# Gated recurrence: score products of a head woven with the output projection of the head in front

## What is computed

```python
def step(S, xs):                      # block by block, per head
    qb, kb, vb, gb = xs
    G = jnp.cumsum(gb, axis=2)
    diff = G[:, :, :, None, :] - G[:, :, None, :, :]
    decay = jnp.exp(jnp.where(tri[:, :, None], diff, -jnp.inf))
    A = jnp.einsum('bhtk,bhsk,bhtsk->bhts', qb, kb, decay)
    o = jnp.einsum('bhts,bhsv->bhtv', A, vb) + jnp.einsum('bhtk,bhkv->bhtv', qb * jnp.exp(G), S)
    ...
    S_new = jnp.exp(G_last[:, :, 0, :])[..., None] * S + jnp.einsum(
        'bhsk,bhsv->bhkv', kb * jnp.exp(G_last - G), vb)
    return S_new, o
...
o = rms_norm(o, norm_g) * jax.nn.silu(g).reshape(B, T, HG_HEADS, HG_VDIM)
out = o.reshape(B, T, D_MODEL).astype(h.dtype) @ w_out
```

## Time and profile before

| | us |
|---|---|
| median of 3 runs | 3793.66 (3791.33 to 3795.40) |
| the profiled execution | 3798.4 |
| its span, from the first to the last instruction | 3796.8 |
| PE busy in the span | 3537.1 (93%) |
| DVE busy | 2125.4 (56%) |
| ACT busy | 1170.7 (31%) |
| score products (L732), first and last start | 120.1 and 878.7 |

### The profile page before, as it was taken

One profiled execution on the slowest core, in us unless ns is written; L12 is line 12 of the kernel. 1 busy time (PEld: TensorE's weight loads), 2 busy tenths in 40 slices (PEclk: granted clock), 3 DMA queues, 4 the chain that ended last, 5 costly groups with the idle time before them and its releaser, 6 DMA issues. The chain is left out here.

```text
span 3796.8 us, 55091 instructions
## 1 busy us (share of the span) xinstructions
PE 3537.1 (93%) x19764; PEld 3151.5 (83%) x19780; DVE 2125.4 (56%) x3935; ACT 1170.7 (31%) x1961; POOL 224.8 (6%) x349
## 2 busy tenths in 40 slices
PE   5999999998999999999978995899989999999997
PEld 4988889886899999999853692454579999999996
DVE  5465555654655545555678776763333555455556
ACT  4222333321411111111335866674433111111112
POOL 3000000000100000000100001100002000000001
PEclk8888888887999999999957996999999999999998
DMA  2110011100111111111201121012431111111111
GB/s 90 35 40 29 29 40 35 40 29 23 36 45 45 40 40 45 45 40 42 88 12 56 74 78 41 12 37 111 177 129 36 48 37 40 45 51 35 40 45 64
DMA packets 57414, 192.33 MB, mean 51 GB/s; under 512 B 7016, under 2 KB 23408, under 8 KB 52528
## 3 DMA queue, kind: packets, MB, share of 16 engines
q1 hardware_dynamic: 52992, 167.89, 12.8%
q0 software_dynamic: 4144, 20.71, 1.5%
HBM read 166.64 MB, written 21.93 MB: 50 GB/s over the span
## 5 line engine op out<-in xcount | busy, mean ns | idle before, releaser
L292 PE MATMUL ff1lin<-ff1h_hi,ff1w_hi 128*128 128x384 f32 x1056 | 354.9, 336 | 10.3 <-DVE ff1w_lo L286 5.7
L292 PE MATMUL ff0lin<-ff0h_hi,ff0w_hi 128*128 128x384 f32 x1056 | 354.1, 335 | 7.3 <-DVE ff0w_lo L286 4.4
L293 PE MATMUL ff1lin<-ff1h_lo,ff1w_hi 128*128 128x384 f32 x1056 | 353.8, 335 | 0.0
L294 PE MATMUL ff1lin<-ff1h_hi,ff1w_lo 128*128 128x384 f32 x1056 | 353.8, 335 | 0.0
L293 PE MATMUL ff0lin<-ff0h_lo,ff0w_hi 128*128 128x384 f32 x1056 | 353.3, 335 | 0.0
L294 PE MATMUL ff0lin<-ff0h_hi,ff0w_lo 128*128 128x384 f32 x1056 | 353.3, 335 | 0.0
L292 PE MATMUL hg_lin<-hg_h_hi,hg_w_hi 128*128 128x384 f32 x768 | 269.6, 351 | 17.3 <-POOL hg_h_lo L165 15.4
L293 PE MATMUL hg_lin<-hg_h_lo,hg_w_hi 128*128 128x384 f32 x768 | 264.4, 344 | 0.0
L294 PE MATMUL hg_lin<-hg_h_hi,hg_w_lo 128*128 128x384 f32 x768 | 263.6, 343 | 0.0
L292 PEld LDWEIGHTS ff1lin<-ff1h_hi,ff1w_hi 128*128 128x128 f32 x1056 | 199.0, 188 | 13.1 <-DVE ff1w_lo L286 6.3
L292 PEld LDWEIGHTS ff0lin<-ff0h_hi,ff0w_hi 128*128 128x128 f32 x1056 | 198.7, 188 | 8.6 <-DVE ff0w_lo L286 4.7
(11 more groups left out here) (429 smaller groups left out, 7807.0 us busy)
## 6 DMA issues: line engine op xcount, KB each, us to landing
ff_raw<-in_weights SPq DMA_DIRECT2D x132, 512.0 KB, 3.3
hg_raw<-in_weights SPq DMA_DIRECT2D x40, 512.0 KB, 3.3
as_keys<-in_cache_k SPq DMA_DIRECT2D x16, 1024.0 KB, 4.8
as_vals<-in_cache_v SPq DMA_DIRECT2D x8, 2048.0 KB, 9.9
se_keys<-in_cache_ki SPq DMA_DIRECT2D x8, 1024.0 KB, 4.8
pb_raw<-in_weights SPq DMA_DIRECT2D x12, 512.0 KB, 3.3
x<-in_x SPq DMA_DIRECT2D x3, 1536.0 KB, 8.7
x_keep<-x POOLq DMA_DIRECT2D x1, 4608.0 KB, 17.4
```

The source lines that it names most:

```text
L292: pe.matmul(out, w_hi, x_hi, start=start, stop=False)
L293: pe.matmul(out, w_hi, x_lo, start=False, stop=False)
L294: return pe.matmul(out, w_lo, x_hi, start=False, stop=stop)
```

## The change

The score products of one chunk are put in a function `attend(c)`, an output unit in `out_unit(n)`, the mask in `mask_scores()`, and one addition in `add_out(n)`. PE no longer runs all score products and then all output units: it takes the score products of two chunks, two output units, and so on eight times; then the 128-column score product of the sample frames, then output units 16 to 23. DVE starts a body with `v_own`, then additions 0 to 5, `w_lo` of the first slab, additions 6 to 15, the mask, and additions 16 to 23. Body 1, which has no output units, and body 9, which has no scores, keep the order on PE. No instruction that computes is added or removed, and every wait keeps its condition.

```diff
             def body(h, par0):
                 r = h - 1
-                if has(h, 1, 9):
+
+                def mask_scores():
                     hold(dve, att_done, r + 1, tk)
...
+                def add_out(n):
+                    nb, g = divmod(n, G)
+                    hold(dve, W.units, units_before(h) + n + 1, tk)
+                    xs = x[:, nb, g * GT:(g + 1) * GT]
+                    dve.tensor_tensor(xs, xs, lin[g][:, 0:GT], ALU.add).then_inc(dve_evac, 1)
+
+                out_here = has(h, 2, 10)
+                if has(h, 1, 9):
                     hold(dve, ss_out, r * 16, tk)
                     dve.tensor_tensor(v_own[:, :, :], spread(vals[:, NT - 1, :].unsqueeze(1), [P, DEC_B, P]),
                                       spread(own_b[:, :].unsqueeze(2), [P, DEC_B, P]), ALU.mult).then_inc(v_spread, 1)
+                if out_here:
+                    dve.drain()
+                    for n in range(6):
+                        add_out(n)
                 if has(h, 0, 8) and body_slabs(h):
                     lo(h, par0, 0)
...
+                if out_here:
+                    for n in range(6, NC):
+                        add_out(n)
+                if has(h, 1, 9):
+                    mask_scores()
+                if out_here:
+                    for n in range(NC, KB * G):
+                        add_out(n)
...
+                out_here = has_out and has(h, 2, 10)
+                for c in range(0, NC, 2):
+                    if has(h, 1, 9):
+                        attend(c)
+                        attend(c + 1)
+                    if out_here:
+                        out_unit(c)
+                        out_unit(c + 1)
+                if has(h, 1, 9):
                     pe.matmul(rb[4][:, 0:P], k_mids[:, :], q_mid[:, T_PROMPT:T], start=True, stop=True).then_inc(att_done, 1)
...
+                if out_here:
+                    for n in range(NC, KB * G):
+                        out_unit(n)
```

More of the change, by code:

```diff
@@ L726, in body @@
                     i.then_inc(turned, 1)
[L727 to L733, removed]
@@ L734, in body, with attend @@
-                    pe.matmul(rb[4][:, 0:P], k_mids[:, :], q_mid[:, T_PROMPT:T], start=True, stop=True).then_inc(att_done, 1)
[L735 to L747, removed]
+                def attend(c):
+                    rows, col = c % 2 * CH, c // 2 * CH
+                    for i_ in range(NS):
+                        n = SB * (i_ + 1)
+                        at = k_at(i_) + c * n
+                        pe.matmul(rb[3][rows:rows + n, col + i_ * SB:col + (i_ + 1) * SB], k_mid[:, at:at + n],
+                                  q_mid[:, c * CH + i_ * SB:c * CH + (i_ + 1) * SB], start=True, stop=True)
@@ new lines, in out_unit @@
+                def out_unit(n):
+                    nb, g = divmod(n, G)
+                    if n == 0:
+                        hold(pe, n_dve, (h - 2) * 2 + 2, tk)
+                        hold(pe, W.lo_done, slab_base(h) + 1, tk)
+                    if n < G and has(h, 2, 9):
+                        hold(pe, act_evac, h * 12 - 2 + n, tk)
+                    else:
+                        hold(pe, dve_evac, (h - 2) * 24 + n - 2, tk)
+                    W.product(pe, lin[g][:, 0:GT], par0, nb * P, o_hi[:, g * GT:(g + 1) * GT],
+                              o_lo[:, g * GT:(g + 1) * GT], True, True).then_inc(W.units, 1)
```

## The result

| | us |
|---|---|
| before, median of 15 runs | 3794.74 (3790.45 to 3801.60) |
| changed, median of 15 runs | 3763.83 (3756.72 to 3786.88) |
| ratio | 0.9928, 95% interval 0.9913 to 0.9942 |
| the changed kernel's profiled execution | 3775.34, span 3773.7 |

The change saves about 31 us by the medians, and 27 us by the ratio, which is one of means and so counts the slower executions of the changed kernel in full. The middle of the forecast was 3759 us, its range 3743 to 3783 us. Two things stand out beside the median. The profiled execution is slower than the median, and the 15 times are spread over 30 us where those of before lie within 11 us: nine are at 3767.6 us or less, four between 3772.4 and 3775.3 us, two at 3783.3 and 3786.9 us.

A forecast was written before the change was run, and what follows sets the result against it. PE bounds the kernel, losing time to waits and half-clock matmuls. Score products 8.3, units 12.7, 128-column product 0.3, turns 1.2, wait 1.8 and joints 0.1 give 24.4 us a body, 35 us saved over seven: 3759 us, range 3743 to 3783 us.

The forecast's parts named there:

- the two leaks: PE's losses in the seven stretches, first score product to first state product: waits (18.55 us) and matmuls at 1.2 GHz.
- The 5 us: Gain per body in the stretch from first score product to first state product: 24.4 us instead of 29.38 us.
- The warm body: One body's stretch with the clock staying at 1.00: 8.3 + 12.7 + 0.3 + 1.2 + 1.8, about 24.4 us.
- The turns: PE's changes between score products and units: 0.15 us per there-and-back, 1.2 us a body, ends 0 and 2.6 us.
- the new wait: PE waits 1.8 us at unit 19 behind DVE's mask, replacing 2.65 us; ends 0 and 2.86 us.
- a cold one: Rival, weave at half clock: 36.5 us a body, 3844 us if all seven; chance 0.08 for most bodies.
- PE enters it from a dense projection at 1.00: Argument against a cold weave: PE comes to the weave from wide work at full clock, read from body 5.
- The rival of one or two cold bodies: One or two of the seven weaves run at half clock: 3771 to 3783 us, chance 0.07.
- `v_own` "with nothing to spare": On DVE ahead of the first addition, needed at unit 3: each 0.1 us later would cost 0.1 us a body.
- The rule that frequent small idles make the clock swing: Skill rule on idles between matmul groups: if the fifteen turns count as such, it foretells the cold weave.
- That the clock would spend the same share at half speed, with the gain in the wait alone: Rival: within the weave the turns (1.2 us) eat the shorter wait's gain (0.85 us): 3796 us, chance 0.05.
- The longer wait with a fall of the clock behind unit 18: Rival: 2.86 us of wait instead of 1.8 us, clock falling in it: body gains 2.5 us, 3776 us.

The follow-up runs named there:

- the grains: Chunks and units per weave step, compared in the changed kernel with its loop written out: steps of two 3752.59 us, steps of four 3747.27 us.
- four and four: Changed kernel with weave steps of four chunks, then four output units, instead of two and two: 3757.14 us looped, 3747.27 us with the loop written out.
- two and two: The changed kernel's own weave steps, two chunks then two output units: 3763.83 us looped, 3752.59 us with the loop written out.
- eight and eight: Changed kernel with weave steps of eight chunks, then eight output units: 3767.97 us, ratio 0.9937 to the kernel before.
- the units-first order: Changed kernel with each step's two output units put ahead of its score products: 3820.19 us; with `v_own` also moved behind addition 9, 3760.41 us.

## Why the prediction came out as it did

**The bound and the two leaks** were read rightly. The span fell by 23.1 us and the stretches by 22.1 us. The 5 us did not come back as a wait later in the body: the pieces between the stretches grew by 2.0 us in all, 0.6 us of it idle at the loop's top, and DVE still waits 1.44 us for the state products.

**The warm body** was forecast at 24.4 us and measured 24.6 us. Term by term: score products 8 x 1.03 = 8.3 us, as forecast. The turns are the difference of the grains, (18.28 - 17.36) / 4 = 0.23 us each with the loop written out, where 0.15 us was taken: 0.6 us a body too little, within its ends. A unit took 0.52 us instead of 0.53 us, the new wait 1.50 us against 1.8 us, and the whole from the 128-column product on 6.30 us against 6.5 us. These errors nearly cancel, and that the sum came out within 0.2 us is luck in part.

**The clock** was forecast rightly for six of seven weaves and in the price of a cold one: 36.5 us forecast, 35.88 us measured. What was mis-sized is its chance. The step that failed is "PE enters it from a dense projection at 1.00". That is true of the earlier trace rows, body 5, and the prediction leaned on that body. Body 4 has an idle of 1.11 us ahead of the transposes in the trace of before, and so a dense projection, an idle, nine transposes and then small products. The prediction named the clock at 0.50 inside a weave as a sign of being wrong, and in body 4 it came. The rival of one or two cold bodies was given 0.07 (3771 to 3783 us); six of 15 executions are at 3772 us or above, and both executions that were profiled had a cold body 4, which accounts for 11.3 of the 11.5 us by which the first lies above the median. The median itself is 4.8 us above the middle of the forecast. Without the six executions at 3772 us and more it would be 3761.6 us, still 2.6 us above; that rest was not traced.

**`v_own` "with nothing to spare"** was noted as a cost of 0.1 us for each 0.1 us. The runs show a step there: a wait of 0.72 us was borne, one of 0.90 us cost 10 us. There was also something to spare: 1.50 us more of DVE's time (1.22 us and the 0.28 us ahead of the next addition) gave waits of 0.62 to 0.91 us away from the loop's top, so some 0.6 us or more had been free. The remark had the right place and the wrong law.

**The two rules of the Trainium skill.** The rule that frequent small idles make the clock swing describes neither the warm nor the cold weave: the fifteen turns alone never brought the clock down (18.28 us at 1.00 in seven weaves of seven when written out), and cold it did not swing but stayed. The rule on long idle gaps does not cover the cold weave, since 29.00 us at 0.50 passed with PE busy throughout.

**The rivals.** That the clock would spend the same share at half speed, with the gain in the wait alone, is refuted by the clock of 1.00 in six of seven weaves and by the 13.2 us of PE's busy time. The longer wait with a fall of the clock behind unit 18 did not occur.

## What to carry to other kernels

Small matmuls woven between wide ones can hold TensorE's clock up and were worth 1% here, but such a weave may run through at either of two speeds: look at the granted clock body by body, not at its mean, and at the spread of the times. Choose the grain so that a run of small work is short enough not to lose the clock and a run of wide work is long enough to win it back; here four and four beat both two and two and eight and eight. Keep idles, even of 1 us, out of the start of the weave, whether they come from another engine or from a loop's branch; where one can't be avoided, put wide work right behind it, as in the run with the units first and `v_own` later, which bore 1.57 us.

## What the runs showed of the hardware

A mixture of 16 score matmuls and six wide ones ran at 1.00 for 18.28 us, and at 0.50 for 29.00 us where the clock had fallen in its first 0.54 us, with the same instructions and PE busy in both. In the scores-first order a wait of 0.62 and one of 0.72 us at unit 3 were borne, and five of 0.90 us and more were not; in the units-first order 0.53 us was borne and 0.62 us was not. A branch back to the top of the loop left PE idle for 1.0 to 1.6 us, which was gone in all four kernels with the bodies written out, and writing six bodies out saved the kernel before 12.7 us. While PE wrote one half of the partitions of a PSUM bank, DVE read the other half for some 0.5 us a body, and neither took longer: PE's run of 32 score products 2.07 us with and without, DVE's four mask instructions 0.87 us with and 0.90 us without.
